# First chunk of a fused adaLN, projection and attention layer: order of ScalarE's and TensorE's early work, one load and one reduction in halves, one rounding on another engine

## What is computed

```python
mod = jax.nn.silu(c) @ w_ada + b_ada
shift, scale, gate = jnp.split(mod, 3, axis=-1)
h = rmsnorm(x, g_norm) * (1.0 + scale[:, None, :]) + shift[:, None, :]
proj = h @ w_in                       # 1024 x 4096
q, k, v, z_attn, b_g, c_g, h_c, z_conv = jnp.split(proj, splits, axis=-1)
q, k = rope(q, positions), rope(k, positions)      # 8 heads of 64
y_attn = rmsnorm(moba_attention(q, k, v), g_attn_out) * jax.nn.silu(z_attn)
y_conv = rmsnorm(short_gated_conv(b_g, c_g, h_c, w_conv), g_conv_out) * jax.nn.silu(z_conv)
x = x + gate[:, None, :] * (jnp.concatenate([y_attn, y_conv], axis=-1) @ w_out)
return rmsnorm(x, g_final)
```

## Time and profile before

| | |
|---|---|
| device time, median of 3 runs | 269.43 us (268.59 to 269.57) |
| the profiled execution | 269.49 us |
| its span, first to last instruction | 267.7 us |
| outside the span | 1.8 us |
| TensorE busy | 257.7 us, 96% of the span |
| VectorE / ScalarE / GpSimd busy | 79% / 51% / 44% |
| first matmul of chunk 0 | at 14.65 us |

### The profile page before, as it was taken

How to read it: one execution, slowest core, us unless ns; L and a number is a source line. 1 busy time by engine, 2 the same in 40 slices (tenths; PEclk the granted TensorE clock), 3 DMA queues, 4 the chain that set the end, 5 groups by cost and what they waited for, 6 DMA issues and landing times.

```text
span 267.7 us, 3634 instructions
## 1 busy us (share of the span) xinstructions
PE 257.7 (96%) x1252; PEld 211.7 (79%) x1252; DVE 210.9 (79%) x337; ACT 137.2 (51%) x230; POOL 116.6 (44%) x71
## 2 busy tenths in 40 slices
PE   4999999999999999999999999999999999999991
PEld 1578888888788888888888888888888888888881
DVE  5799999799999976969969675924495569999554
ACT  5875576646097533591644723556927751310543
POOL 3410000558333433093366332337667975590440
PEclk9999999999999999999999999999999999999998
DMA  6999996698604642049463112532842592000034
GB/s 204 400 418 428 413 423 234 233 339 230 220 2 157 154 160 82 0 151 369 115 174 121 51 45 78 157 82 78 250 143 81 205 413 86 3 0 0 23 138 157
DMA packets 13220, 46.96 MB, mean 175 GB/s; under 512 B 2065, under 2 KB 2705, under 8 KB 11922
## 3 DMA queue, kind: packets, MB, share of 16 engines
q1 hardware_dynamic: 12912, 46.46, 49.8%
q10 hardware_dynamic: 290, 0.27, 0.3%
HBM read 40.43 MB, written 2.10 MB: 159 GB/s over the span
## 4 chain that ended last, share of the span: by engine, by line
PE 91%; DMA 2%; ACT 1%; POOL 1%; issue 1%; SPq 1%; DVE 0%; POOLq 0%
PE ps L1105 22%; PE ps L1107 22%; PE ps L1106 22%; PE ps L1190 5%; PE ps L1267 3%; PE ps L1255 3%; PE ps L1213 2%; PE ps L1205 2%; DMA xt<-in_x 2%; PE ps L1211 2%; PE ps L1203 2%; PE ps L1281 2%; PE ps L1274 2%; ACT x_junk L339 1%; POOL w_hi L639 1%
## 5 line engine op out<-in xcount | busy, mean ns | idle before, releaser
L645 POOL TENSOR_TENSOR w_lo<-raw,w_hi 128x1024 fp32r<-128x1024 f32 x29 | 75.0, 2596 | 104.5 <-ACT w_hi L361 69.2
L1105 PE MATMUL ps<-h_lo,w_hi 128*128 128x512 f32 x200 | 79.0, 395 | 0.0
L1107 PE MATMUL ps<-h_hi,w_hi 128*128 128x512 f32 x200 | 78.0, 390 | 0.0
L1106 PE MATMUL ps<-h_hi,w_lo 128*128 128x512 f32 x200 | 77.9, 390 | 0.0
L1107 PEld LDWEIGHTS ps<-h_hi,w_hi 128*128 128x128 f32 x200 | 37.5, 188 | 8.0
L1105 PEld LDWEIGHTS ps<-h_lo,w_hi 128*128 128x128 f32 x200 | 37.5, 188 | 7.9
L1106 PEld LDWEIGHTS ps<-h_hi,w_lo 128*128 128x128 f32 x200 | 37.6, 188 | 7.4
L361 ACT ACTIVATE w_hi<-raw 128x1024 fp32r<-128x1024 f32 x29 | 30.4, 1051 | 3.1 <-DMA raw<-in_wslots 3.1
L451 ACT ACTIVATE probs<-probs,rmin 128x384 f32<-128x384 f32 (+3 forms) x32 | 17.6, 550 | 14.0 <-DVE rmin L898 14.0
L908 DVE TENSOR_SCALAR probs<-probs,prec 128x384 f32<-128x384 f32 (+3 forms) x32 | 20.7, 709 | 0.3
L898 DVE CUSTOM_DVE_ANT_0 probs<-mask,ps 128x384 f32<-128x384 f32 (+3 forms) x32 | 13.4, 483 | 4.3 <-PE ps L1255 4.3
(11 more groups left out here) (158 smaller groups left out, 486.2 us busy)
## 6 DMA issues: line engine op xcount, KB each, us to landing
raw<-in_wslots SPq DMA_DIRECT2D x33, 512.0 KB, 3.4
ada<-in_ada SPq DMA_DIRECT2D x10, 1024.0 KB, 11.8
raw<-in_whead SPq DMA_DIRECT2D x7, 448.0 KB, 9.8
xt<-in_x SPq DMA_DIRECT2D x4, 512.0 KB, 5.8
ada<-in_ada SPq DMA_DIRECT2D x4, 512.0 KB, 8.3
qd<-qt SPq DMA_DIRECT2D x16, 128.0 KB, 2.3
kd<-kt SPq DMA_DIRECT2D x16, 128.0 KB, 2.3
x<-in_x SPq DMA_DIRECT2D x4, 512.0 KB, 5.8
```

The source lines that it names most:

```text
L645: nc.gpsimd.tensor_tensor(lo, src[:, :], hi.bitcast(F32), ALU.subtract).then_inc(s_lo, 1)
L1105: nc.tensor.matmul(o, a_hi, b_lo, start=start, stop=False)
L1106: nc.tensor.matmul(o, a_lo, b_hi, start=False, stop=False)
L1107: return nc.tensor.matmul(o, a_hi, b_hi, start=False, stop=stop)
```

## The change

Five edits, all in front of or inside chunk 0:

1. ScalarE squares the last x tile before it takes the two sines, not after.
2. The load of part 0 of `ada[0]` is issued as two loads of 512 columns each. Its reduction is done in two halves too (`mod_first`), the first ahead of VectorE's scaling of x tile 2; the first half's sum goes to `part` and is the start of the second's.
3. v's 512 weight columns of chunk 0 are rounded by ScalarE, between `gs[0]` and `h_hi[0]`; the other 384 stay with GpSimd (own semaphore `hw_hi0r`).
4. ScalarE copies the tables out of PSUM after the two halves of `h_hi[0]`, ahead of `h32`, not before all of them. The cosine table goes through bank 7, not 3, and `keep_warm` through bank 6.
5. TensorE transposes the sine table after x tile 2, and the cosine table after x tile 3; two `keep_warm` (256 and 128 columns) are gone, and in chunk 0 the C matmul, whose bank is the cosine table's, comes last.

```diff
 # SyncE
-            for two in range(2):
-                sp.dma_start(ada[0][:, two, :], ada0_d[two]).then_inc(a01_in[two], 16)
+            for half in range(2):
+                cols = slice(half * BANK, (half + 1) * BANK)
+                sp.dma_start(ada[0][:, 0, cols], ada0_d[0][:, cols]).then_inc(a0_in[half], 16)
+            sp.dma_start(ada[0][:, 1, :], ada0_d[1]).then_inc(a01_in[1], 16)
 # ScalarE
             square_x(2)
+            square_x(3)
             act.wait_ge(angle, angle_steps)
...
-            square_x(3)
...
-            act.wait_ge(trig_tr, 1)
-            nc.scalar.activation(sin_t[:, :], bank(2), ACT.Copy, scale=prm[:, C_SIGN:C_SIGN + 1]).then_inc(trig_ok, 1)
-            act.wait_ge(trig_tr, 2)
-            nc.scalar.activation(cos_t[:, :], bank(3), ACT.Copy).then_inc(trig_ok, 1)
...
+                if j == 0:
+                    act.wait_ge(hw0_in, 16)
+                    nc.scalar.activation(w_hi[0][:, 0:BANK], raw[0][:, 0:BANK], ACT.Copy).then_inc(hw_hi0, 1)
...
+                    act.wait_ge(trig_tr, 1)
+                    nc.scalar.activation(sin_t[:, :], bank(2), ACT.Copy, scale=prm[:, C_SIGN:C_SIGN + 1]
+                                         ).then_inc(trig_ok, 1)
+                    act.wait_ge(trig_tr, 2)
+                    nc.scalar.activation(cos_t[:, :], bank(7), ACT.Copy).then_inc(trig_ok, 1)
 # GpSimd
-            for lo, hi in ((0, BANK), (BANK, HEAD_W)):
...
-                nc.gpsimd.tensor_copy(w_hi[0][:, lo:hi], src[:, lo:hi]).then_inc(hw_hi0, 1)
+            pool.wait_ge(arrived, count)
+            nc.gpsimd.tensor_copy(w_hi[0][:, BANK:HEAD_W], src[:, BANK:HEAD_W]).then_inc(hw_hi0r, 1)
 # VectorE
+            def mod_first(half):
+                cols = slice(half * BANK, (half + 1) * BANK)
+                dve.wait_ge(a0_in[half], 16)
+                dve.wait_ge(cb_ok, half + 1)
+                if half:
+                    dve.wait_ge(mod_part, 1)
+                dve.tensor_tensor_reduce(mod_junk[:, cols], ada[0][:, 0, cols], c_bc[:, cols], 1.0,
+                                         part[:, :] if half else 0.0, ALU.mult, ALU.add,
+                                         acc[:, 0:1] if half else part[:, :]).then_inc(mod_step if half else mod_part, 1)
+
+            mod_first(0)
             scale_x(2)
-            mod_half(0, 0)
+            mod_first(1)
             mod_half(0, 1)
 # TensorE
                         if m < TT - 1:
-                            if m == 2:
-                                table(0)
-                                table(1)
                             pe.wait_ge(x_norm, m + 1)
                         else:
-                            keep_warm(2 * P)
-                            keep_warm(P)
+                            table(0)
...
                 ins.then_inc(x_tr, 1)
+                if j == 0:
+                    table(1)
...
                     pe.wait_ge(hw_hi0, 1)
-                    pe.wait_ge(trig_ok, 2)
                     pe.wait_ge(cb_ok, 2)
                     pe.wait_ge(hhi_half, 1)
-                    order = (2, 3, 4, 5, 6, 0, 1)
+                    order = (2, 3, 4, 5, 0, 1, 6)
...
-                    if j == 0 and n == 6:
-                        pe.wait_ge(hw_hi0, 2)
                     if j == 0 and n == 0:
+                        pe.wait_ge(hw_hi0r, 1)
                         pe.wait_ge(rows_ok, 1)
+                    if j == 0 and n in (1, 6):
+                        pe.wait_ge(trig_ok, 1 if n == 1 else 2)
```

More of the change, by code:

```diff
@@ L156, in build @@
         gs, sh, b1 = sb("gs", [KT]), sb("sh", [KT]), sb("b1", [KT])
-        acc = sb("acc", [KT])
+        acc, part = sb("acc", [KT]), sb("part", [1])
         gcol = sb("gcol", [KT])
@@ L175, in build @@
         hw0_in, rows_tr, rows_ok, x_col = sem("hw0_in"), sem("rows_tr"), sem("rows_ok"), sem("x_col")
+        a0_in, mod_part, hw_hi0r = [sem(f"a0_in{i}") for i in range(2)], sem("mod_part"), sem("hw_hi0r")
         a01_in = [sem(f"a01_in{i}") for i in range(4)]
@@ L747, in mod_half @@
                     dve.wait_ge(a01_in[2 * j + two], 16)
-                    if j == 0:
-                        dve.wait_ge(cb_ok, 2)
                 else:
@@ L801, in _ @@
                         mod_half(j, two)
-                dve.wait_ge(hw_hi if j else hw_hi0, j if j else 2)
+                if j:
+                    dve.wait_ge(hw_hi, j)
+                else:
+                    dve.wait_ge(hw_hi0, 1)
+                    dve.wait_ge(hw_hi0r, 1)
                 nc.vector.tensor_tensor(w_lo[j % 4][:, 0:HEAD_W], raw_place(j)[0][:, 0:HEAD_W],
@@ L1118, in keep_warm @@
             def keep_warm(w):
-                nc.tensor.matmul(bank(7, 0, w), ident[:, :], mask[:, 0:w], start=True, stop=True)
+                nc.tensor.matmul(bank(6, 0, w), ident[:, :], mask[:, 0:w], start=True, stop=True)
             keep_warm(BANK)
             def table(n):
-                b, src = ((2, sin_k), (3, cos_k))[n]
+                b, src = ((2, sin_k), (7, cos_k))[n]
                 pe.wait_ge(trig_k, n + 1)
```

## The result

The changed kernel takes 270.3 us (median of 7 runs, 269.7 to 270.98), the kernel before 268.9 in the same comparison (7 runs, 268.3 to 269.57): 1.0052 times as long, 95% interval 1.0031 to 1.0074. It is slower, by a little over half a per cent, where 269.2 was forecast. The time lies inside the stated range, 268.5 to 270.5, but it moved the other way than forecast: the direction is that of the rival, a late rise of TensorE's rate.

What follows compares the result with a forecast made beforehand. The prediction took TensorE alone to bound the kernel from chunk 0's start, which waits for h. Starting chunk 0 0.25 us earlier gave 269.49 - 0.25 = 269.24 us, other edits hidden; range 268.5 to 270.5.

Steps and rivals of the forecast that it cites:

- What bounds the kernel: Whole kernel: TensorE alone from chunk 0's first matmul at 14.65 to 259.15 us; h releases chunk 0.
- The floor under the loads: Loads before chunk 0: parts 0 and 1 of `ada[0]` land at 11.0 and 12.3 us, unharmed by the added issue.
- the split: First reduction in halves on VectorE: `acc[0]` ready at about 12.2 as before, shift at 13.6 instead of 13.68, gain 0.1 us.
- the rounding: v's first weights on ScalarE before chunk 0: 0.62 us, ready at 13.5, hidden before the shift; nothing gained on the path.
- the copies of the tables: ScalarE after `h_hi`: two copies of 0.6 us, a stall of 0 to 0.1, `h32` at about 16.55, cost nothing.
- `h_hi` and chunk 0's start: Before chunk 0: `h_hi`'s first half starts at 13.68 instead of 13.94, so chunk 0 starts at 14.39, 0.25 us earlier.
- the 0.25: Chunk 0's start: the forecast gain in us, taken whole from the time of the kernel before.
- The signs of being wrong: TensorE: transposes still 0.21 us apart at 13, or chunk 0's first matmuls more than 0.3 us apart, among others.
- TensorE's rate rises later: TensorE idle before x tile 2, so high rate comes late, each us at half rate costing 0.5; slower, chance 0.28.
- Its middle: Late-rate rival's middle case: rate rises at 15.7, +0.15 for chunk 0's start and +0.45 at half rate, 270.1 us.
- No change: Rival: the 0.25 at chunk 0 goes in late `h32`, the wait for `cos_t`, or rounding of 0.96; 269.5 us, chance 0.15.
- a larger gain: Rival: chunk 0 did wait for GpSimd's casts, and its inner gaps go too; 268.9 us, chance 0.07.

## Why the prediction was wrong

- **What bounds the kernel** held. TensorE never waits after chunk 0's start, and what chunk 0 lost, the span lost: 1.07 us at chunk 1, 1.0 in the span.
- **The floor under the loads, the split, the rounding, the copies of the tables** held to 0.2 us each in the trace: landings 10.4 and 12.3, `acc[0]` ready at 12.06, shift ready at 13.63, rounding 12.96 to 13.59. `h32` came at 16.72, 0.17 later than worked out, and VectorE waited 0.32 for it, off the path.
- **The failed step** is in the part on `h_hi` and chunk 0's start: "transposes done by 13.4 to 13.8, so `h_hi`'s first half starts at about 13.68 in place of 13.94, and chunk 0 at 13.68 + 0.57 + 0.14 = 14.39". This needed TensorE at its high rate by then. The transposes ended at 13.84, `h_hi` started at 13.96, and the queue of TensorE (cosine table, `keep_warm`) at half rate lasted to 15.5, not 14.8 as the rival had it: from 13.63, the last x transpose's place in the chain, to 15.55. Nothing of the 0.25 was gained. The signs of being wrong that the prediction named both came: four transposes took 0.85, 0.21 apart, at 12.8, and chunk 0's first matmuls were 0.43 apart.
- **The rival** "TensorE's rate rises later" was what happened, with 0.28 given to it. Its middle, 270.1, was made of a start 0.15 later and a rise at 15.7; measured in the profiled execution were a fifth matmul 1.06 later and a rise at 16.4. Its sum was too small by its own terms: from x tile 2 on the queue has 14 transposes, not 13, and the last `keep_warm` takes 0.85 us at the low rate (the chain above), not 0.43. From 11.5 that gives 15.3 for its end, a start 0.65 later than before, and about 270.3 for the middle. That the measured 270.3 stands so close to 270.1 is partly luck: it holds 0.4 us outside the span that the rival had not, and in the comparison the kernel before took 268.9, not the 269.49 of the sum. Filling the gap took the loss in the span away, and the one edit that makes a gap without the rest (the square) cost 2.4 us. Its weight was too small because I took it that the rate would rise as long after the idle stretch as it had after 10.23, at 14.3; it rose at 16.4. The Trainium skill (TensorE: Matmul & The Clock Gate, The HAM clock gate) says that the throttled state is the default and that the moment of the rise differs from run to run. The traces agree with the second: of the kernels with the gap filled, one is at the high rate by 11.07 and another only by 13.55.
- **A term was missing altogether:** about 0.35 us outside the span, which comes with the reduction in halves; two other instructions in VectorE's program put 0.2 to 0.25 us there. The sum took the 1.8 us outside the span as a constant. Without this term the ratio would have stayed under half a per cent.
- **"No change" and "a larger gain"** did not occur. That the old casts were not what chunk 0 waited for was right: with halves and rounding alone the median of 11 spans was 267.5, that of the kernel before.

## What to carry to other kernels

Before moving a small operation ahead on one engine, look at what TensorE does in the time that its results now come later: idle stretches of 0.65 to 1.5 us in the run-up cost the gain hoped for, 0.25 us, several times over. Filler paid here where it filled the idle stretch ahead of the transposes, and not where it stood ahead of the one-row matmuls. Filler is free as long as another engine is late, and on the path as soon as TensorE is. When a change of tenths of a microsecond is measured, compare the time outside the span too: for one kernel it stayed within 0.13 us (1.75 to 1.88), and it moved by 0.35 here for a reason that no view of the span shows.

## What the runs showed of the hardware

- The granted clock read 1.00 in each microsecond from 9 to 17 of the changed kernel (below, two windows: length, busy times, granted clock, DMA), the level of 2.4 GHz, while its matmuls of 512 columns started 0.43 us apart in the first of them and 0.22 in the second, the pace of 1.2 and of 2.4 GHz. In these traces the pace has to be read from the starts.

```profile
15.00:16.00 1.00, 1.00 (x4) 0.81 (x3) 1.00 (x2) 1.00 (x3) 0.00 (x0) 1.00 1.02 413
16.00:17.00 1.00, 1.00 (x5) 0.77 (x5) 0.68 (x3) 1.00 (x3) 0.00 (x0) 1.00 1.13 459
```

- Two more instructions in VectorE's program put 0.2 to 0.35 us outside the span, one did not (one memset 1.75, two 2.05, one small reduction 2.05; 2.1 to 2.2 for all kernels with the reduction in halves). What happens there is not seen in any view.
- A cast of 384 columns by GpSimd took 0.51 us both before, with the 512-column cast of 1.23 us right ahead of it, and after, without it.
